# A ring of twenty value rows in the last group of a gathering encoder layer

## The reference, cut to what matters

```python
def run(blk):
    xc, ec, gc = blk                      # 128 tokens, their 128 experts, their gates
    u = jnp.take(w_u, ec, axis=0)
    h = jnp.einsum('cd,ced->ce', xc, u, preferred_element_type=jnp.float32)
    a = (jax.nn.gelu(h, approximate=False) * gc).astype(x.dtype)
    return jnp.einsum('ce,ced->cd', a, jnp.take(w_v, ec, axis=0))
```

## Time and profile before

| | us |
|---|---|
| median of 3 runs | 3568.05 |
| lowest, highest | 3566.01, 3570.0 |
| the profiled execution | 3567.75 |
| its span, from the first to the last instruction | 3565.9 |
| TensorE busy in it | 2630.8 |
| VectorE, ScalarE, GpSimd busy | 2230.6, 1609.0, 2132.8 |

### The profile page before, as it was taken

How to read it: one execution, slowest core, us unless ns; L and a number is a source line. 1 busy time by engine, 2 the same in 40 slices (tenths; PEclk the granted TensorE clock), 3 DMA queues, 4 the chain that set the end, 5 groups by cost and what they waited for, 6 DMA issues and landing times.

```text
span 3565.9 us, 40329 instructions
## 1 busy us (share of the span) xinstructions
PE 2630.8 (74%) x14180; PEld 2145.1 (60%) x14180; DVE 2230.6 (63%) x5046; ACT 1609.0 (45%) x1839; POOL 2132.8 (60%) x2063
## 2 busy tenths in 40 slices
PE   7999966787887665778896766778887755555555
PEld 4467655566766664656765655667756654444444
DVE  5242277887656766777656766776566675666643
ACT  2111024555554454555544454555554454444444
POOL 1000046777766666777766667777766666666665
PEclk9999987888998986888998987888988976666667
DMA  6013389999999999999999999999999999999998
GB/s 218 25 71 104 124 319 371 355 356 364 409 409 407 401 382 356 362 351 376 409 409 405 399 372 356 371 342 398 409 407 396 383 365 367 359 366 364 366 365 310
DMA packets 341758, 1219.29 MB, mean 342 GB/s; under 512 B 37874, under 2 KB 47091, under 8 KB 341172
## 3 DMA queue, kind: packets, MB, share of 16 engines
q0 software_dynamic: 294912, 1073.87, 78.8%
q1 hardware_dynamic: 34980, 118.92, 9.1%
q10 hardware_dynamic: 11664, 23.92, 1.8%
HBM read 1204.25 MB, written 12.32 MB: 341 GB/s over the span
## 4 chain that ended last, share of the span: by engine, by line
PE 25%; POOL 20%; issue 15%; another core or an unknown queue 11%; DMA 11%; DVE 9%; ACT 7%; DVEq 2%; ACTq 0%; POOLq 0%
POOL rows L369 10%; POOL rows L360 10%; PE acc L733 8%; DMA rows<-in_peer_u,ids_peer 6%; ACT rows L1311 5%; DMA rows<-in_peer_v,ids_peer 4%; DVE rows L1052 4%; PE mB L658 2%; PE fA L601 2%; PE fA L559 2%; PE fA L624 1%; PE mB L577 1%; PE fB L624 1%; PE fB L398 1%
## 5 line engine op out<-in xcount | busy, mean ns | idle before, releaser
L733 PE MATMUL acc<-ident,rows 128*128 128x128 f32 x8192 | 1331.3, 319 | 757.2 <-issue 471.4
L733 PEld LDWEIGHTS acc<-ident,rows 128*128 128x128 f32 x8192 | 1142.6, 166 | 960.0 <-issue 612.3
L1311 ACT ACTIVATE rows<-rows,coef 128x1024 f32<-128x1024 f32 x1024 | 1149.6, 1144 | 897.9 <-DMA rows<-in_peer_v,ids_peer 702.3
L360 POOL DMA_INDIRECT rows<-in_peer_u,ids_peer x1024 | 1051.1, 1026 | 679.3 <-DVE ids_peer L1032 315.0
L369 POOL DMA_INDIRECT rows<-in_peer_v,ids_peer x1024 | 1062.9, 1038 | 604.4 <-remote 260.3
L1052 DVE CUSTOM_DVE_ANT_0 rows<-rows,fB 128x1024 f32<-128x1024 f32 x538 | 649.9, 1216 | 408.6 <-DMA rows<-in_peer_u,ids_peer 316.9
L1052 DVE CUSTOM_DVE_ANT_0 rows<-rows,hh 128x1024 f32<-128x1024 f32 x486 | 587.4, 1221 | 259.6 <-DMA rows<-in_peer_u,ids_peer 188.7
L658 PE MATMUL mB<-hT_g,wring 128*128 128x256 f32 x1024 | 241.1, 388 | 5.8 <-issue 4.6
L601 PE MATMUL fA<-hT_g,wring 128*128 128x256 f32 x1024 | 241.2, 390 | 4.7 <-issue 4.5
L601 PEld LDWEIGHTS fA<-hT_g,wring 128*128 128x128 f32 x1024 | 196.9, 196 | 33.3 <-issue 7.2
L658 PEld LDWEIGHTS mB<-hT_g,wring 128*128 128x128 f32 x1024 | 196.4, 197 | 33.2 <-issue 6.9
(11 more groups left out here) (203 smaller groups left out, 2262.1 us busy)
## 6 DMA issues: line engine op xcount, KB each, us to landing
wring<-in_wstream SPq DMA_DIRECT2D x192, 512.0 KB
rows<-in_peer_u,ids_peer POOLq DMA_INDIRECT x1024
rows<-in_peer_v,ids_peer POOLq DMA_INDIRECT x1024
hT_spill<-rows ACTq DMA_DIRECT2D x1, 4096.0 KB
wring<-in_wstream SPq DMA_DIRECT2D x16, 256.0 KB
hT_g<-hT_spill ACTq DMA_DIRECT2D x4, 1024.0 KB
out_h<-ybuf ACTq DMA_DIRECT2D x8, 512.0 KB
S<-in_w_lat SPq DMA_DIRECT2D x1, 2048.0 KB, 12.8
```

The source lines that it names most:

```text
L360: pool.indirect_dma_start(u_rows[:, ring(g, i, NU), :], None, peer_u, bass.IndirectOffsetOnAxis(ap=ids_peer[:, t, s:s + 1], axis=0)).then_ ...
L733: last = mm(acc[:, tok(k)], v_rows[:, ring(g, i, NV), tok(k)], ident[:, :], is_transpose=True, start=i % SLOTS == 0 and k % 4 == 0, stop=i ...
L1311: s.activation(row, row, ACT.Copy, scale=coef[:, b, i % BATCH:i % BATCH + 1]).then_inc(scaled, 1)
```

## The change

In the last group the ring of v rows has twenty places: the eight of before, then the eight rows of `KT`, then four rows that each take two blocks of `V`. Places 8 to 19 are used for the first time without a wait for `v_free`, since nothing stands in them; the first of these gathers waits for `w_free` instead. From slot 20 on, a gather waits for slot i - 20.

```diff
+NVL = NV + 12
...
+        def v_row(g, i):
+
+            r = i % NVL if g == GROUPS - 1 else ring(g, i, NV)
+            if r < NV:
+                return v_rows[:, r, :]
+            if r < NV + H:
+                return KT[:, r - NV, :]
+            r = 2 * (r - NV - H)
+            return V[:, r:r + 2, :].rearrange("p a b -> p (a b)")
+
+        def v_sem(g, i):
+
+            return v_in[i % NVL if g == GROUPS - 1 else ring(g, i, NV)]
+
+        def v_landed(g, i):
+
+            if g < GROUPS - 1:
+                return landed(g, i, NV)
+            before = g * STEPS // NV if i % NVL < NV else 0
+            return 16 * (before + i // NVL + 1)
...
             def gather_v(g, i):
                 g, i = slot_of(g, i)
 
-                pool.wait_ge(v_free, g * STEPS + i + 1)
+                if g == GROUPS - 1 and i >= NVL:
+                    pool.wait_ge(v_free, NV + g * STEPS + i - NVL + 1)
+                elif g == GROUPS - 1 and i >= NV:
+                    if i == NV:
+                        pool.wait_ge(w_free, used(g, WP0 - 1))
+                else:
+                    pool.wait_ge(v_free, g * STEPS + i + 1)
                 t, s = divmod(i, SLOTS)
                 pool.indirect_dma_start(
-                    v_rows[:, ring(g, i, NV), :], None, peer_v,
-                    bass.IndirectOffsetOnAxis(ap=ids_peer[:, t, s:s + 1], axis=0)).then_inc(v_in[ring(g, i, NV)], 16)
+                    v_row(g, i), None, peer_v,
+                    bass.IndirectOffsetOnAxis(ap=ids_peer[:, t, s:s + 1], axis=0)).then_inc(v_sem(g, i), 16)
```

More of the change, by code:

```diff
@@ L258, in layer_program @@
         u_in = [sem(f"u_landed{i}") for i in range(NU)]
-        v_in = [sem(f"v_landed{i}") for i in range(NV)]
+        v_in = [sem(f"v_landed{i}") for i in range(NVL)]
         u_free, scaled, y_read = sem("u_free"), sem("scaled"), sem("y_read")
@@ L732, in peer @@
                 for k in range(KD):
-                    last = mm(acc[:, tok(k)], v_rows[:, ring(g, i, NV), tok(k)], ident[:, :], is_transpose=True,
+                    last = mm(acc[:, tok(k)], v_row(g, i)[:, tok(k)], ident[:, :], is_transpose=True,
                               start=i % SLOTS == 0 and k % 4 == 0, stop=i % SLOTS == SLOTS - 1, skip_group_check=True)
@@ L1307, in scale @@
                     act.wait_ge(coef_done, g * (STEPS // BATCH) + i // BATCH + 1)
-                act.wait_ge(v_in[ring(g, i, NV)], landed(g, i, NV))
+                act.wait_ge(v_sem(g, i), v_landed(g, i))
                 b = i // BATCH % 2
-                row = v_rows[:, ring(g, i, NV), :]
+                row = v_row(g, i)
                 s.activation(row, row, ACT.Copy,
```

## The result

The changed kernel takes 3586.69 us (median of 5 runs, 3582.66 to 3596.43), the kernel before 3568.05 in the same comparison: a ratio of 1.0063, 95% interval 1.0051 to 1.0075. It is 18.6 us slower, beyond the predicted range (3490 to 3582).

The account below looks back on a forecast made before the run. GpSimd's issue of gathers, stopped only by its wait on v_free, was taken to bound the last group. Lead -2, pace -3 and drain +8 gave +3 us: 3568.05 + 3 = 3571 us, range 3490 to 3582.

Parts of the forecast that it names:

- Three things say that GpSimd's own pause ends it: Last group: TensorE's slow single matmuls end only after GpSimd stops gathering, 0.20 us per gather, 3.46 us behind 16 gathers.
- Rival A: Last group: TensorE's lateness is its own; a deeper ring removes all 96 us of stall; 3494 us, chance 0.22.
- B: Last group: some freed rows still get through, stalls once in 20 slots, 36 us stay; middle 3535 us, chance 0.16.
- C: Last group: DMA is full with gathers alone, so removing GpSimd's stall gives nothing; 3570 us, chance 0.07.
- The budget of before: Last group: 480 gathers at 0.943 + 0.305 us plus 96 us of v stall make 695 against 694.2 us.
- terms 1 and 2: Last group: one-time lead of a longer first run of gathers, -2 us, and pace after it, -3 us.
- part (e): GpSimd's queue: order unchanged, v gather i still precedes u gather i+16, and the u ring keeps six rows.
- part (d): Scalings and transposes read KT or V in place of the ring: same shape, 1.15 and 1.1 to 2.0 us, no new wait.
- term 3: End of the last group: up to 12 more slots left before the end, 0 to +15.2 us, taken as +8.
- Rival D: Last group: TensorE falls 12 slots further behind, all after the last gather, +15.2 us; 3583 us, chance 0.17.
- The signs: Last group: v idle near 165 us, rate near 364 GB/s, TensorE ending 15 us or more after last gather's start.
- satisfied, 0 us: V gather 8 of the last group waits on w_free for the last output-projection weight, 77 steps earlier; 0 us.

## Why the prediction was wrong

**Right: the jam needs GpSimd's pause.** The step "Three things say that GpSimd's own pause ends it" held in the runs of a jamming chip that kept their transposes. Its 0.20 us per gather came back as a pace of 1.44 us a gather with a longer step, with narrow rows and with the ring of twenty (its late stalls are 3.38 to 3.41 us for 16 gathers). With half the transposes it was 0.17, and without them, behind VectorE's lists, nothing was owed. Rival A needed the stalls to vanish; they only moved. B and C are out with it: what stays is not 36 us, and DMA moves 410 GB/s.

**The step that failed: stalls were counted before v gathers only.** The budget of before, with all stalls in front of L369, was right, and rival A's argument says it in words: "the u ring never holds GpSimd". The sum for the change took this over. Its terms 1 and 2 (-5 us together) price v gathers, part (e) notes only that "the u ring keeps six rows", and part (d) says "no new wait"; a stall before a u gather stood at nothing, without a reason. Measured, it is +46.0 us on u against -28.5 on v, so the two terms should have been +17.5 and not -5. The pause is owed whatever the ring, so rows that make the v wait rarer only let TensorE be later, and what is late next is ScalarE's eviction (26.26 us), the Gelus and the sum behind it, the dots, the u rows. The pace between the two places was indeed that of before (slots 24 to 128: 300.8 us, before 301.6).

**Drain, term 3:** +8 taken, +6.3 measured; the size is luck. The prediction took six slots more at 1.27 us each; it was ten slots more (17 against 7) at 0.89 us, in part beside scalings that still ran. With the ring of twelve it is 19.8 us, as before. Rival D had a good part of the picture: TensorE falls further behind, and its sign, six more slots outstanding at the last gather, came true. But its 3583 comes near the time by the wrong sum: it put all 15 us behind the last gather, and three quarters of the loss are ahead of it.

**The signs.** The idle before v gathers was to stay near 165 us and is 143.1, the rate near 364 GB/s and is 355, and TensorE was to end 15 us or more after the last gather's start and ends 15.0 after it. They were signs for the pause, and they held in the main; none of them looked at u.

**Two figures of the prediction** don't follow from its own terms: bounds of -9.8 and +15.2 give 3558 to 3583 and not 3561 to 3578, and C with term 3 halved is 3572 and not 3570. The measured time lies above the range by either.

**The claims "satisfied, 0 us"** for the weights' wait and "no new wait" for scaling in KT and V held: the v gather of slot 8 has the fixed gap of 0.30 us before it, the u stalls name VectorE, and on a free chip the kernel is equal to within 0.13%.

**Against the Trainium skill** (DMA: Bandwidth & Descriptors, Where 436 GB/s comes from): the page's limit of about 358 GB/s from HBM lies near the 364 of the jamming chips, and by it no ring could help. The traces disagree: windows with 410 and 405 GB/s speak against it as the cause, and 230 GB/s at the same 1.445 us a gather exclude it.

**Still open:** which resource GpSimd's gathers share with the short instructions of TensorE and VectorE; whether it is GpSimd's issuing or the number of packets (the narrow rows had as many, 128 a gather, with fewer bytes); why the freed row is signalled some three slots after its transposes; and why some chips are free of it. Of the kernels that still give the reference's output none beat the kernel before on either sort of chip.

## What to carry to other kernels

Here a deeper ring only moved a wait. It removes one only if what is waited for comes by itself; if the waiting engine's pause is what lets the other catch up, more rows turn a short wait at one engine into a long one at several. So when a ring is to be deepened, follow the late engine's other customers (evictions, turns, whatever is queued behind them) to the next ring, and price that. A stall whose length goes with the run of work before it, at a constant sum per item, is a debt and not slack.

## What the runs showed of the hardware

- On three jamming chips, gathers at 1.245 us slow the short instructions of TensorE (0.7 to 3.5 us apart) and VectorE (0.97 to 2.45 us gaps) until GpSimd has paused, 3.4 us behind 16 gathers; over such a cycle a gather costs 1.42 to 1.445 us, with u rows of 1 KB as with 4 KB. Long instructions (dots 1.22 us, scalings 1.15) and GpSimd's own gathers keep their length.
- On three other chips the kernel before runs 4.5% faster (3407 against 3567 us). It left no trace there; the traces of the changed kernel and of the variants there show no jam.
- A memset of 16 floats between two gathers costs GpSimd nothing: it lies in the fixed gap.
- DMA engines moved 410 GB/s for 100 us while gathers were issued every 1.245 us, and 329 GB/s when GpSimd waited for an earlier landing before each v gather.
